# Last stage of a decoder layer: weights through the experts' buffers, bias as one fp32r product, transposes within a tile

## The reference

```python
for e in range(N_EXPERTS):
    hid = jax.nn.silu(u @ w_gate_e[e]) * (u @ w_up_e[e])
    y = y + combine[..., e:e + 1] * (hid @ w_down_e[e])
...
v = rmsnorm(h, g_ple)
h = h + jax.nn.sigmoid(v @ w_ple_gate + b_ple_gate) * (p @ w_ple_proj)
out = rmsnorm(h, g_final)
```

## Time and profile before

| | |
|---|---|
| median of 3 runs | 1613.49 us (1611.84 to 1614.65) |
| profiled execution | 1611.33 us, its span 1609.6 us |
| TensorE busy in the span | 1404.6 us (87%) |
| VectorE, ScalarE busy | 761.4 us (47%), 629.1 us (39%) |
| expert stage ends, last stage starts | about 1423 us |
| last stage | 1423 to 1609.6 us |

### The profile page before, as it was taken

The page is one execution under the profiler, slowest core; times in us unless marked ns, Lnnn a source line. Parts: engine busy times, 40 slices in busy tenths (PEclk is TensorE's granted clock), DMA queues, the critical chain, the costliest instruction groups (busy, mean ns, idle before and its releaser), DMA issues. The chain is left out here.

```text
span 1609.6 us, 24113 instructions
## 1 busy us (share of the span) xinstructions
PE 1404.6 (87%) x7996; PEld 1169.7 (73%) x7997; DVE 761.4 (47%) x1240; ACT 629.1 (39%) x930; POOL 148.6 (9%) x146
## 2 busy tenths in 40 slices
PE   4999999638999999999859973999999999728997
PEld 3777889636999898888738863777877777516774
DVE  6632112335544444344244325668655767636552
ACT  5211210113333334454333311567654656514442
POOL 0000000013111113223000000000100000011000
PEclk9999999868999999999959985999999999958999
DMA  5123321243000122242043313979976979564310
GB/s 187 56 71 97 111 79 30 50 107 80 21 21 21 36 46 54 53 98 65 22 138 118 107 64 138 346 275 383 345 248 239 368 271 374 194 234 157 130 54 39
DMA packets 107988, 222.48 MB, mean 138 GB/s; under 512 B 14749, under 2 KB 41405, under 8 KB 107910
## 3 DMA queue, kind: packets, MB, share of 16 engines
q1 hardware_dynamic: 96950, 183.07, 34.9%
q0 software_dynamic: 7488, 27.27, 4.7%
q10 hardware_dynamic: 3472, 11.09, 1.7%
HBM read 176.56 MB, written 36.24 MB: 132 GB/s over the span
## 5 line engine op out<-in xcount | busy, mean ns | idle before, releaser
L1169 ACT ACTIVATE att_prob<-att_ps_s 128x512 f32<-128x512 f32 (+1 forms) x240 | 134.7, 562 | 246.3 <-PE att_ps_s L1096 201.4
L1218 DVE TENSOR_REDUCE att_mx<-att_ps_m 128x1 f32<-128x512 f32 (+3 forms) x256 | 132.9, 560 | 135.0 <-PE att_ps_m L1043 123.3
L1915 DVE TENSOR_TENSOR moe_g_lo<-moe_g_raw,moe_g_hi 128x1024 fp32r<-128x1024 f32 x128 | 148.2, 1220 | 44.7 <-ACT moe_g_hi L1835 44.7
L134 PE MATMUL moe_ps_g<-moe_g_hi,moe_xT_hi 128*128 128x512 f32 x336 | 137.6, 410 | 17.0 <-DVE moe_g_lo L1915 16.8
L1835 ACT ACTIVATE moe_g_hi<-moe_g_raw 128x1024 fp32r<-128x1024 f32 x128 | 125.0, 1048 | 43.3 <-PE moe_ps_g L136 27.7
L1114 PE MATMUL att_ps_o<-tok_vsw,att_prob 128*128 128x65 f32 x1056 | 140.2, 274 | 0.0
L135 PE MATMUL moe_ps_g<-moe_g_lo,moe_xT_hi 128*128 128x512 f32 x336 | 133.9, 399 | 0.0
L136 PE MATMUL moe_ps_g<-moe_g_hi,moe_xT_lo 128*128 128x512 f32 x336 | 133.7, 398 | 0.0
L1114 PEld LDWEIGHTS att_ps_o<-tok_vsw,att_prob 128*128 128x128 f32 x1056 | 131.3, 192 | 2.6 <-ACT att_prob L1169 0.5
L134 PE MATMUL prj_ps_w<-prj_hT_hi,prj_w_hi 128*128 128x512 f32 x256 | 103.2, 403 | 3.0 <-DVE prj_w_lo L405 3.0
L136 PE MATMUL prj_ps_w<-prj_hT_hi,prj_w_lo 128*128 128x512 f32 x256 | 100.4, 392 | 0.0
(11 more groups left out here) (339 smaller groups left out, 2920.4 us busy)
## 6 DMA issues: line engine op xcount, KB each, us to landing
moe_g_raw<-in_w_gate_e SPq DMA_DIRECT2D x128, 256.0 KB, 4.7
moe_g_raw<-in_w_up_e SPq DMA_DIRECT2D x128, 256.0 KB, 5.7
moe_d_raw<-in_w_down_e SPq DMA_DIRECT2D x64, 512.0 KB
y_rows<-moe_y ACTq DMA_DIRECT2D x21, 512.0 KB, 6.0
prj_w_raw<-in_w_in SPq DMA_DIRECT2D x16, 512.0 KB, 4.0
att_q_raw<-feat SPq DMA_DIRECT2D x32, 256.0 KB, 4.1
feat<-prj_feat POOLq DMA_DIRECT2D x14, 512.0 KB, 2.9
att_k_raw<-feat SPq DMA_DIRECT2D x24, 256.0 KB, 4.9
```

Of the source, the lines that this page charges most:

```text
L134: nc.tensor.matmul(out, a_hi, b_hi, start=first, stop=False)
L1169: nc.scalar.activation(prob[:, b % PT, 0:w], ps_s[:, b % ST, 0:w], ACT.Exp, scale=-1.0).then_inc(expd, 1)
L1218: last = nc.vector.tensor_reduce(mx[i % 2][:, col, q:q + 1], p[:, at:at + (kb - ka) * P], X, ALU.min)
L1915: nc.vector.tensor_tensor(g_lo[:, ch % GR], g_raw[:, ch], g_hi[:, ch % GR].bitcast(F32), ALU.subtract).then_inc(s_glo, 1)
```

## The change

The buffers for weights, `h`, `p` and the gain g_ple now live in a scope `exp` around both stages. SyncE loads the gain, four tiles of rows and the last stage's weights behind the last expert's; the weights go into `g_raw` (gate, 8 chunks) and the first two chunks of `d_raw` (projection). ScalarE and VectorE split the first four chunks at the end of the expert stage, the other six at the start of the last stage ahead of head(0), followed on ScalarE by a square root of a constant. The gathered rows, `v`, the gate, the output and the last gain lie in the raw buffers that are free by then. The bias is split in two rows, high and low, at partitions 0 and 1, and added by one fp32r product with two rows of ones. TensorE transposes tile t+1 after the first 24 products of tile t instead of ahead of them. The stage's semaphores are partly in `exp`, whose exit comes after the last stage's.

```diff
@@ stage_moe, SyncE
                 load_d(sp.value_load(K["texp"][0:1, bass.ds(end + 1, 1)], min_val=0, max_val=NE - 1), o)
+                sp.dma_start(K["gain_ple"][:], a["g_ple"].to_broadcast((P, D))).then_inc(T["vec_in"], 16)
+                for t in range(HB):
+                    sp.dma_start(K["h"][:, t, :], T["h"][t]).then_inc(T["h_in"][t], 16)
+                    sp.dma_start(K["p"][:, t, :], p_d[t]).then_inc(T["h_in"][t], 16)
                 for ch in range(GC):
-                    wait_alone(sp, g_in[ch], o * 32 + 32, ended)
+                    sp.wait_ge(s_ghi, o * GC + (ch + 1))
+                    sp.wait_ge(s_glo, o * GC + (ch + 1))
+                    sp.dma_start(g_raw[:, ch].rearrange("p m n -> p (m n)"), wl_d[ch]).then_inc(g_in[ch], 16)
+                for ch in range(KP):
+                    sp.wait_ge(s_dhi, o * DC + (ch + 1 + DC))
+                    sp.wait_ge(s_dlo, o * DC + (ch + 1 + DC))
+                    sp.dma_start(d_raw[:, ch, :], wp_d[ch]).then_inc(d_in[ch], 16)
@@ stage_moe, ScalarE
                 new_d(end, False)
+                o = place(act, end + 1)
+
+                def last_split(ch):
+                    act.wait_ge(g_in[ch], o * 32 + 48)
+                    nc.scalar.activation(g_hi[:, ch], g_raw[:, ch], ACT.Copy).then_inc(last_hi, 1)
+
+                for ch in range(EARLY):
+                    last_split(ch)
                 y_copy(end)
@@ stage_moe, VectorE
                 new_d(end)
+                for ch in range(EARLY):
+                    dve.wait_ge(last_hi, ch + 1)
+                    nc.vector.tensor_tensor(g_lo[:, ch], g_raw[:, ch], g_hi[:, ch].bitcast(F32), ALU.subtract)
@@ stage_finish, SyncE
-                sp.dma_start(gain[:], a["g_ple"].to_broadcast((P, D))).then_inc(vec_in, 16)
-                sp.dma_start(gfin[:], a["g_final"].rearrange("(a n) -> a n", a=1).to_broadcast((P, D))).then_inc(vec_in, 16)
-                sp.dma_start(bgate[:], a["b_ple_gate"]).then_inc(vec_in, 16)
+                sp.dma_start(b_raw, a["b_ple_gate"]).then_inc(bias_in, 16)
+                sp.wait_ge(split_lo, KD - EARLY)
+                sp.dma_start(gfin, a["g_final"].rearrange("(a n) -> a n", a=1).to_broadcast((P, D))).then_inc(final_in, 16)
...
-                rows(0)
-                for k in range(KD + KP):
-                    if k >= WR:
-                        sp.wait_ge(split_lo, k - WR + 1)
-                    sp.dma_start(w_raw[:, k % WR, :], wg_d[k] if k < KD else wp_d[k - KD]).then_inc(w_in[k % WR], 16)
-                    if k < HB - 1:
-                        rows(k + 1)
+                sp.wait_ge(bias_lo, 1)
+                sp.dma_start(b_two[0:1, :].bitcast(F32), b_hi.bitcast(F32)).then_inc(bias_two, 16)
+                sp.dma_start(b_two[1:2, :].bitcast(F32), b_lo.bitcast(F32)).then_inc(bias_two, 16)
@@ stage_finish, tiles
+                split()
                 head(0)
                 turn(0)
+                bias()
                 head(1)
-                split()
@@ stage_finish, ScalarE and VectorE
-                    for k in range(KD + KP):
-                        act.wait_ge(w_in[k % WR], 16 * (k // WR + 1))
-                        nc.scalar.activation(w_hi[:, k, :], w_raw[:, k % WR, :], ACT.Copy).then_inc(split_hi, 1)
+                    for k in range(EARLY, KD + KP):
+                        nc.scalar.activation(weight("hi", k), weight("raw", k), ACT.Copy).then_inc(split_hi, 1)
+                    nc.scalar.activation(first_root[:], K["c"][:, K_ONE:K_ONE + 1], ACT.Sqrt)
+
+                def bias():
+                    act.wait_ge(bias_in, 16)
+                    nc.scalar.activation(b_hi, b_raw, ACT.Copy).then_inc(bias_hi, 1)
...
+                def bias():
+                    nc.vector.tensor_copy(ones, K["c"][0:2, K_ONE:K_ONE + P]).then_inc(ones_set, 1)
+                    dve.wait_ge(bias_hi, 1)
+                    nc.vector.tensor_tensor(b_lo, b_raw, b_hi.bitcast(F32), ALU.subtract).then_inc(bias_lo, 1)
@@ stage_finish, TensorE
                 turn(0)
                 for t in range(NT):
-                    if t + 1 < NT:
-                        turn(t + 1)
                     pe.wait_ge(v_lo, 3 * t + 3)
...
+                            if ks[0] == 0 and h == 0 and t + 1 < NT:
+                                turn(t + 1)
                             if ks[0] == 0:
-                                last = nc.tensor.matmul(out_[:, h, :], K["c"][0:1, K_ONE:K_ONE + P], bgate[:, r],
-                                                        start=False, stop=True)
+                                if t == 0:
+                                    pe.wait_ge(ones_set, 1)
+                                    pe.wait_ge(bias_two, 32)
+                                last = nc.tensor.matmul(out_[:, h, :], ones, b_two[:, r], start=False, stop=True)
```

More of the change, by code:

```diff
@@ L1694, in _, with expert_buffers @@
                 last.then_inc(named, 1)
+def expert_buffers(sc, K, T):
+    for name, shape, dt in (("g_raw", [P, KD, 2, FE], F32), ("d_raw", [P, KF, D], F32), ("g_hi", [P, KD, 2, FE], F32R),
+                            ("g_lo", [P, KD, 2, FE], F32R), ("d_hi", [P, KF, D], F32R), ("d_lo", [P, KF, D], F32R),
+                            ("h", [P, HB, D], F32), ("p", [P, HB, PLE], F32), ("gain_ple", [P, D], F32)):
+        K[name] = sc.sb(name, shape, dt)
+    T["h_in"] = [sc.sem(f"h_in{i}") for i in range(HB)]
+    T["vec_in"] = sc.sem("vec_in")
 def stage_moe(nc, a, K, T):
@@ L1709, in stage_moe @@
     with Scope(nc, "moe") as sc:
[L1710 to L1715, removed]
+        g_raw, d_raw, g_hi, g_lo, d_hi, d_lo = (K[n] for n in ("g_raw", "d_raw", "g_hi", "g_lo", "d_hi", "d_lo"))
         xg = sc.sb("xg", [P, D])
@@ L2046, in stage_finish, with weight @@
     with Scope(nc, "fin") as sc:
[L2047 to L2053, removed]
+        free = K["g_raw"][:].rearrange("p k m n -> p (k m n)")
+        ys = free[:, 0:4 * D].rearrange("p (a k n) -> p a k n", a=2, k=2)
+        vt, gate, ot, gfin = (free[:, n * D:(n + 1) * D] for n in range(4, 8))
+        EARLY = 4
+        b_raw, b_hi, b_lo = K["d_raw"][0:1, 2, :], K["d_hi"][0:1, 2, :], K["d_lo"][0:1, 2, :]
+        b_two, ones = K["d_hi"][0:2, 3, :], K["d_lo"][0:2, 3, 0:P]
+        ht, pt, gain = K["h"], K["p"], K["gain_ple"]
+        first_root = sc.sb("first_root", [P, 1])
+        def weight(part, k, r=slice(0, D)):
+            if k < KD:
+                return K[f"g_{part}"][:, k].rearrange("p m n -> p (m n)")[:, r]
+            return K[f"d_{part}"][:, k - KD, r]
         junk = sc.sb("junk", [P, D], BF16)
@@ L2114, in _, with tiles @@
                                                 ).then_inc(y_in[t % 2], 16)
-            def tiles(head, turn, weigh, tail, split):
+            def tiles(head, turn, weigh, tail, split, bias):
+                split()
                 head(0)
                 turn(0)
+                bias()
                 head(1)
-                split()
                 for i in range(NT + 1):
@@ L2168, in tail @@
                     nc.scalar.activation(rt[:, t, 1:2], rt[:, t, 1:2], ACT.Sqrt).then_inc(f_root, 1)
-                tiles(head, turn, weigh, tail, split)
+                tiles(head, turn, weigh, tail, split, bias)
             @block.vector
@@ L2220, in tail @@
                     dve.wait_ge(mixed, t + 1)
[L2221 removed]
+                    nc.vector.tensor_tensor(h, h, gate, ALU.add).then_inc(added, 1)
                     dve.wait_ge(f_sq, t + 1)
@@ L2229, in tail @@
                         dve.wait_ge(o_out, 16 * t)
-                    nc.vector.scalar_tensor_tensor(ot[:], h, rs[:, t, 1:2], gfin[:], ALU.mult,
+                    else:
+                        dve.wait_ge(final_in, 16)
+                    nc.vector.scalar_tensor_tensor(ot, h, rs[:, t, 1:2], gfin, ALU.mult,
                                                    ALU.mult).then_inc(o_made, 1)
-                tiles(head, turn, weigh, tail, split)
+                tiles(head, turn, weigh, tail, split, bias)
             @block.tensor
@@ L2308, in build @@
         stage_route(nc, K, T)
-        stage_moe(nc, a, K, T)
-        stage_finish(nc, a, K, T, out)
+        with Scope(nc, "exp") as exp:
+            expert_buffers(exp, K, T)
+            stage_moe(nc, a, K, T)
+            stage_finish(nc, a, K, T, out)
 _INS = ["x", "p", "positions", "g_mix", "w_in", "b_nsa_gate", "b_forget", "pe_cmp_k", "w_cmp_k1", "w_cmp_k2",
```

53 lines of the change are left out of this document (26 added, 27 removed).

## The result

The changed kernel takes 1624.35 us in the median (1619.32 to 1629.43) where the kernel before, on the same chip, takes 1611.78 (1608.69 to 1614.65): a ratio of 1.0077 [1.0054, 1.0101], 12.6 us more. Two further comparisons gave 1.0062 [1.0045, 1.0080] and 1.0062 [1.0033, 1.0091]. The change makes the kernel slower by 0.6 to 0.8%. The forecast was 1614.0, with a range up to 1621.0: the median lies 3.4 us past its end.

What follows compares the result with a forecast made beforehand. TensorE bounds the last stage after an idle start; a new 20.2 us loop and five clock losses of 1.9 us give back the gains: span 1610.1, 0.5 over 1609.6, so 1613.49 + 0.5 = 1614.0; range 1607.5 to 1621.0.

Steps and rivals of the forecast that it cites:

- A loop through ScalarE's written order: Last stage, tiles 1 to 6: later transposes delay ScalarE's sigmoid, which TensorE's next tile awaits; 20.2 us a tile, was 17.39.
- the start's gain: Start of last stage: early loads and splits let tile 0 start at 1440.5 against 1452.91, 12.4 us earlier.
- the bias's gain: Last stage's bias products on TensorE: the replacement product saves 2.04 us a tile, 1.64 if at 0.43.
- The first rival: TensorE stays the bound in the last stage: tiles of 15.35 us, 33.3 us less, 1580.2; chance 0.06.
- The second rival: The loop is there but the clock stays up: 9.0 us less, 1604.5; chance 0.08.
- part 2: Bias product in the last stage: takes 0.23 us instead of f32's 1.05, saving 2.04 us a tile.
- the loop's length: Last stage, tiles 1 to 6: 5.52 us of products plus 14.66 from transposes to sigmoid's end, 20.2 us, five times.
- the clock, 4.1 us slow and 1.9 us lost a gap: TensorE behind each of five loop gaps of 4.9 us: clock falls to 0.50 for 4.1 us, losing 1.9 us.
- The third rival: Clock comes back late: slow stretches of 7 us cost 3.25 us a gap, 7.3 us more, 1620.8; chance 0.18.
- the cold start: Tile 0's first 24 products in the last stage: 5.52 us plus 1.9 for the slow clock, ending at 1447.9.
- the store, priced at 0: Experts' store at 1419.2 could queue behind late weight loads: priced at 0, upper bound 2 us.
- a wrong cover: Early loads hidden in the expert stage, landed by about 1417; a last-stage first DMA after 1424 would disprove it.

Runs made afterwards that it cites:

- e2: The changed kernel with transposes within a tile for tile 0 alone, ahead of the products from tile 1 on: 1589.01 us, ratio 0.9854 to before.
- e6: e2 with the fp32r bias product over 128 rows, 126 of them zero, instead of two: 1585.50 us, ratio 0.9840 to before.
- e4: The changed kernel plus fifteen unused 128x512 products into a spare PSUM bank behind tiles 1 to 5: 1609.98 us, ratio 0.9986 to before.
- e5: e2 with the bias again as one plain float32 product of one row: 1600.66 us, ratio 0.9932 to before.
- e3: The kernel before with only the transposes moved behind a tile's first 24 products: 1628.00 us, ratio 1.0105 to before.
- after_third: The changed kernel measured a third time, nothing altered: ratio 1.0062 [1.0033, 1.0091] to before.
- before_again: The kernel before measured once more, nothing altered: ratio 0.9982 [0.9961, 1.0004] to before.

## Why the prediction was off

**The mechanism was right.** A loop through ScalarE's written order takes the bound from TensorE, the gap takes the clock down every time, and the start's gain and the bias's gain are given back. By the forecast's own marks: the first product 17.6 us after the stage's first DMA (17.4 said); ScalarE's copies of a tile over 20 us apart; TensorE waiting for the sigmoid before tiles 2 to 6; the clock down behind each wait. The first rival, TensorE staying the bound, is dead for the changed kernel, and e2 with 1589.0 and e6 with 1585.5 are what it would have been with another place for the transposes (the rival had 1580.2).

**The second rival**, the loop at full clock, was put at 1604.5; e4 makes it by force and takes 1610.0. The difference lies in the terms below other than the clock, the longer loop and TensorE's own work above all.

**Failed: part 2, "I take 0.23, since weights and bias are now of one kind".** One kind is not enough: the number of rows changed too. Against the old product's three distances (0.32, 1.06 and 0.34, 1.72 in sum) the new ones take 1.09: 0.63 saved a product, 1.26 a tile, not 2.04; between e5 and e2 it is 1.2. Even the bound taken from 0.43, 1.64 a tile, was too good, as it put the distance behind the bias at 0.23, which stayed at 0.34. 2.0 a tile is right for e6 alone. This counts only where TensorE's own work sets the time: the rest of tile 0, tile 6 and tile 7. There the measured times against the forecast's are: from the transposes of tile 1 to tile 1's first product 10.73 against 9.83 (+0.9), tile 6 19.15 against 17.25 (+1.9, of which 0.9 is the clock's), tile 7 15.2 against 14.26 (+0.9). That is 2.8 us without the clock, the largest of the stage's terms; some 0.8 us of each is the bias product. Inside the loop the shorter work would only have made the gap longer.

**Failed in size: the loop's length, 20.2 us.** At full clock it is 20.51 (e4): 5.67 us from a tile's first product to the transposes where 5.52 was said, and 14.83 for 14.66. Over five tiles this is 1.6 us, the whole of the difference in the way from tile 1's first product to tile 6's, 110.2 us against 108.6.

**Nearly right: the clock, 4.1 us slow and 1.9 us lost a gap.** Behind the five gaps the products' distance goes from 0.43 to 0.23 after 3.7, 5.6, 3.1, 4.9 and 6.1 us, mean 4.7. The first half of a tile takes 7.2, 8.2, 7.1, 8.0 and 8.4 us (tiles 2 to 6), where e4 has 5.67: 2.1 us lost a gap. In the first four gaps it is 1.9, as said; the fifth loses 2.8. The fifteen slow stretches of the changed kernel's three profiles last 2.7 to 6.1 us. The third rival, 7 us in each gap and 1620.8 in all, was the nearest of all to the result, but by luck: no stretch lasted 7 us and no gap lost its 3.25. At the cold start tile 0's first half took 8.24 against 7.4. The rule of the Trainium skill that spoke against the change, "TensorE: Matmul & The Clock Gate", section "HAM oscillation", says that waits between bursts of products bring the clock down again for each burst. The changed kernel agrees: gaps of 4.0 us, fifteen falls in fifteen over three profiles. In e3 it is borne out only once: four of its five gaps of 2.8 us brought none.

**Failed: the store, priced at 0.** It was 0.25 to 1.5 us in the changed kernel, within the bound of 2 us, and 2.6 in e5. The forecast had the early loads landed by 1417; they kept the DMA engines full until about 1421 in after_third and past 1424 in the first profile. The forecast's mark for a wrong cover, a first DMA later than 1424, was met with 1428.87, but 4.3 of these us came from upstream.

**The sum.** The stage came out at 193.8 us where the forecast's numbers give 1610.1 - 1423.1 = 187.0: 6.8 more (start 0.2, tile 0's first half 0.8, TensorE's own work in the rest of tile 0 and in tiles 6 and 7 2.8, the loop's length 1.6, the clock 0.9, the end 0.5). With 1.5 at the store and 4.3 upstream it is the 12.6 us between the span of 1622.7 and the forecast's 1610.1. The upstream part was no term of the forecast and is mostly chance; without it the forecast would still have been 8.3 us low, as it was in the two further comparisons (1622.05 and 1622.60 us against 1614.0). The range had room for the store and the bias, yet not for these with a longer loop, a longer cold start and a stage that starts late by itself: single profiles of one kernel differ by 4 us in where it starts.

## What to carry to other kernels

Before an instruction is moved later on one in-order engine, follow who stands behind it in the written order of the others: where the last of them releases the first engine again, the move closes a loop, and its length (here 14.8 us plus the work moved ahead) is the new period however short each engine's work is. Put the moved step inside only the turn where nobody waits yet, as in e2. Where a product of a few rows stands among products of 128, try it with the rows of its neighbours, even if they are zeros; here that paid 0.8 us a tile.

## What the hardware showed that was not expected

- A product of 2 rows among fp32r products of 128 rows costs 0.63 us where one of 128 rows costs 0.23: the distances around it are 0.32, 0.43 and 0.34 instead of 0.23 each.
- A gap of 4.0 us brought the clock down in fifteen of fifteen cases (the changed kernel's three profiles), one of 2.8 us in one of five (e3), while 2.54 us did so in the expert stage. The slow stretch behind the 4.0 us gaps lasts 2.7 to 6.1 us and isn't the same twice in a row.
- The clock can fall amid short waits too, and not in each execution: in tile 0 of before with no wait over 0.98 us, in before_again not, with one of 1.89. It made 2.6 us of the stage.
- Products into a spare bank in such a gap keep the clock up and made the kernel 12 us faster.
